# Attention scores from rounded parts, and one weight loaded a stage earlier into a place of its own

## What is computed

```python
ss = jnp.einsum('bghqd,bgqkd->bghqk', qb, kg) + bias_s      # selected keys
osel = jnp.einsum('bghqk,bgqkd->bghqd', masked_softmax(ss, ...), vg)
sw = jnp.einsum('bghqd,bgkd->bghqk', qb, kwb) + head_bias(rel_w)   # window keys
ow = jnp.einsum('bghqk,bgkd->bghqd', masked_softmax(sw, ...), vwb)
```

## Time and profile before

| what | value |
|---|---|
| median of 3 runs | 2342.91 us (2341.49 to 2344.74) |
| the profiled execution: its own time | 2339.77 us |
| its span, first to last instruction | 2337.7 us |
| granted TensorE clock, mean over the span | 0.986 of full |
| PE busy, share of the span | 95% |
| attention stage's 48 steps | about 783 to 931 us |
| state-space stage and what follows it | from 1183 us |
| mixture of experts | from about 1380 us to the end |

### The profile page before, as it was taken

How to read it: one execution, slowest core, us unless ns; L and a number is a source line. 1 busy time by engine, 2 the same in 40 slices (tenths; PEclk the granted TensorE clock), 3 DMA queues, 4 the chain that set the end, 5 groups by cost and what they waited for, 6 DMA issues and landing times. The chain is left out here.

```text
span 2337.7 us, 32450 instructions
## 1 busy us (share of the span) xinstructions
PE 2226.8 (95%) x13844; PEld 1652.4 (71%) x13844; DVE 820.4 (35%) x1668; ACT 504.4 (22%) x885; POOL 210.0 (9%) x173
## 2 busy tenths in 40 slices
PE   8999999999999998999989999999999999998987
PEld 5888888888888777878877876555565555555553
DVE  6453245243225688453256561111111111111113
ACT  3221333231223554242224220000000000000001
POOL 0640000011100000750000000000000000000000
PEclk9999999999999999999999999999999999999999
DMA  8633222354331100435163689999999999999997
GB/s 260 231 122 126 72 85 91 100 167 151 116 96 28 42 24 27 175 124 167 59 129 127 250 344 409 427 426 427 427 426 427 427 427 426 427 426 427 428 426 313
DMA packets 123829, 573.29 MB, mean 245 GB/s; under 512 B 30488, under 2 KB 44428, under 8 KB 97784
## 3 DMA queue, kind: packets, MB, share of 16 engines
q1 hardware_dynamic: 110468, 533.21, 58.2%
q0 software_dynamic: 12064, 33.79, 4.1%
q10 hardware_dynamic: 1152, 4.19, 0.5%
HBM read 543.63 MB, written 39.47 MB: 249 GB/s over the span
## 5 line engine op out<-in xcount | busy, mean ns | idle before, releaser
L525 PE MATMUL ps<-w_parts,u_parts 128*128 128x512 f32 (+2 forms) x1920 | 414.6, 376 | 2.9 <-DVE u_parts L713 2.6
L525 PEld LDWEIGHTS ps<-w_parts,u_parts 128*128 128x128 f32 x1920 | 349.2, 188 | 61.2 <-DVE u_parts L713 3.1
L3254 PE MATMUL ps<-mem,mem_u 128*64 128x256 f32 x2464 | 291.4, 390 | 4.5 <-issue 2.8
L490 DVE TENSOR_TENSOR w_parts<-w_raw,w_parts 128x2048 fp32r<-128x2048 f32 (+2 forms) x70 | 161.8, 2311 | 321.1 <-ACT w_parts L485 321.1
L3377 DVE TENSOR_TENSOR mem_c<-mem_c,ps 128x256 f32<-128x256 f32 x64 | 26.9, 421 | 684.9 <-PE ps L3254 678.7
L3254 PEld LDWEIGHTS ps<-mem,mem_u 128*64 128x64 f32 x2464 | 181.2, 135 | 110.2 <-issue 17.1
L485 ACT CAST w_parts<-w_raw 128x2048 fp32r<-128x2048 f32 (+2 forms) x70 | 128.6, 1837 | 399.4 <-PE ps L525 166.3
L3281 PE MATMUL ps<-mem,mem_c 128*64 128x512 f32 x624 | 194.7, 625 | 20.1 <-DMA mem<-in_expert_w_down 11.2
L1569 PE MATMUL ps<-w_parts,u_parts 128*128 128x512 f32 x768 | 181.6, 393 | 0.4 <-DVE u_parts L1598 0.4
L1569 PEld LDWEIGHTS ps<-w_parts,u_parts 128*128 128x128 f32 x768 | 142.2, 188 | 29.8 <-issue 0.8
L523 PE MATMUL ps<-u_parts,w_parts 128*128 128x512 f32 x672 | 154.5, 390 | 1.7 <-DVE w_parts L490 1.7
(11 more groups left out here) (447 smaller groups left out, 2675.3 us busy)
## 6 DMA issues: line engine op xcount, KB each, us to landing
mem<-in_expert_w_gate SPq DMA_DIRECT2D x39, 2048.0 KB, 35.6
mem<-in_expert_w_up SPq DMA_DIRECT2D x38, 2048.0 KB, 40.7
mem<-in_expert_w_down SPq DMA_DIRECT2D x37, 2048.0 KB, 40.9
mem_u<-in_expert_w_up SPq DMA_DIRECT2D x26, 2048.0 KB, 40.5
mem_u<-in_expert_w_down SPq DMA_DIRECT2D x19, 2048.0 KB, 42.1
mem_c<-in_expert_w_gate SPq DMA_DIRECT2D x13, 2048.0 KB, 36.0
mem_u<-in_expert_w_gate SPq DMA_DIRECT2D x12, 2048.0 KB, 36.6
w_raw<-in_od_w_in SPq DMA_DIRECT2D x21, 1024.0 KB, 5.1
```

What stands on the lines that cost most here:

```text
L490: dve.tensor_tensor(self.part(n, 1), self.raw(n), self.part(n, 0).bitcast(F32), ALU.subtract).then_inc(self.low, 1)
L525: mm = pe.matmul(out, u[:, x, ku, g.t * P:(g.t + 1) * P], w[y][:, kk, :], start=first, stop=last)
L3254: mm = pe.matmul(ps[SLOTS * h:SLOTS * (h + 1), bank, 0:256].rearrange("s (c j) -> s c j", j=2), x[:, kk, :], w[:, kk, :].rearrange("p (c h ...
```

## The change

Two parts.

**Attention.** The scores of heads 1 to 11, tiles 1 to 3, are made from rounded parts, three products each, where they were one float32 matmul. ACT rounds the four key matrices once, in step 0's turn, and each next head's queries in the turn of t=1; DVE makes the low parts, the keys' in step 1's turn, the queries' in the turn of t=2. For steps with t<2, ACT copies both transposed halves in one instruction, and DVE's copy is left out.

**Fourier output weight.** Chunk 4 gets a place of its own (`N0`), and SP issues its load in `ssm` right after the lag tables, ahead of the wait for `ft_ok`. The table `dft` moves to another free place. In `mix_mid` the copies of the state-space sums and the rounding of the weight take turns, on ACT and on DVE.

```diff
     def slot(self, n):
+        if n == FOURIER_CHUNK:
+            return N0
...
                     for i, kT in enumerate((k.ksT, k.kwT)):
-                        pe.matmul(k.ps[:, 2 * (u % 2) + i, 0:m], k.qT[:, h, t * P:(t + 1) * P], kT[:, g, 0:m],
-                                  start=True, stop=True).then_inc(scored, 1)
+                        if h == 0 or t == 0:
+                            mm = pe.matmul(o, k.qT[:, h, t * P:(t + 1) * P], kT[:, g, 0:m], start=True, stop=True)
+                        else:
+                            pe.wait_ge(k_low, 2 * NKV)
+                            pe.wait_ge(q_low, h)
+                            for x, z in PRODUCTS:
+                                mm = pe.matmul(o, q_parts[x][:, h % 2, t * P:(t + 1) * P],
+                                               k_parts[z][:, NKV * i + g, 0:m], start=x + z == 0, stop=x == 1)
+                        mm.then_inc(scored, 1)
...
             def take_turned(v):
-                act.wait_ge(turned, 2 * v + 1)
+                both = steps[v][1] < 2
+                act.wait_ge(turned, 2 * v + 1 + both)
...
+                if both:
+                    act.copy(pT[v % 2].rearrange("p (i w) -> p i w", i=2)[:, :, 0:w], k.ps[:, 4:6, 0:w]).then_inc(cop_a, 1)
...
                     exponential(u, 1)
+                    if u == 0:
+                        split_keys()
+                    if t == 1 and h + 1 < NH:
+                        split_head(h + 1)
...
+                    if u == 1:
+                        for i, kT in enumerate((k.ksT, k.kwT)):
+                            for g in range(NKV):
+                                dve.wait_ge(k_high, NKV * i + g + 1)
+                                dve.tensor_tensor(k_parts[1][:, NKV * i + g, :], kT[:, g, :],
+                                                  k_parts[0][:, NKV * i + g, :].bitcast(F32), ALU.subtract).then_inc(k_low, 1)
+                    if t == 2 and h + 1 < NH:
+                        dve.wait_ge(q_high, h + 1)
+                        dve.tensor_tensor(q_parts[1][:, (h + 1) % 2, :], k.qT[:, h + 1, :],
+                                          q_parts[0][:, (h + 1) % 2, :].bitcast(F32), ALU.subtract).then_inc(q_low, 1)
-                if 2 <= u < n + 2:
+                if 2 <= u < n + 2 and steps[u - 2][1] >= 2:
...
-    waves, dft = view(k, k.slot(first + 1) + 2048, NT, S), view(k, k.misc + 2080, 2 * P)
+    waves, dft = view(k, k.slot(first + 1) + 2048, NT, S), view(k, k.slot(first + 1), 2 * P)
...
                 sp.dma_start(T[SC * j:SC * (j + 1), :, :], kk[:, :, SC * (L - 1 - j):SC * (2 * L - 1 - j)]).then_inc(t_in, 16)
+            load_weights(k, sp, "ssm", first + 1)
             sp.wait_ge(ft_ok, 1)
...
             act.copy(ft[0], k.FT).then_inc(ft_high, 1)
-            k.last_sums(act)
             wait_chunk(k, act, first)
             for kk in range(4):
+                k.last_sum(act, kk)
                 act.copy(w4[0][:, kk, :], raw[0][:, kk, :]).then_inc(w4_high, 1)
...
-            k.last_sums_by_dve(dve)
...
+            k.last_sum_by_dve(dve, 0)
+            for kk in range(3):
+                k.last_sum_by_dve(dve, kk + 1)
+                four_low(kk)
+            four_low(3)
```

More of the change, by code:

```diff
@@ L66 @@
 ROUTE = Z0 + 16640
+FOURIER_CHUNK = 4
 def shape_constants():
@@ L1920, in nsa @@
     bias_loaded = [k.sem(f"nsa_bias{i}") for i in range(2)]
+    q_high, q_low, k_high, k_low = (k.sem("nsa_" + x) for x in ("q_high", "q_low", "keys_high", "keys_low"))
+    q_parts = [rounded(k, f"nsa_q_{x}", N0 + 1024 * i, 2, S) for i, x in enumerate(("high", "low"))]
+    k_parts = [rounded(k, f"nsa_keys_{x}", o, 2 * NKV, S) for x, o in (("high", Z0 + 11264), ("low", Z0 + 8192))]
+    PRODUCTS = ((0, 0), (0, 1), (1, 0))
     c_uses = [("score", t) for t in range(NT)]
@@ L1926, in nsa, with by_dve @@
             ("mix", 0): 11, ("turn", 2): 12, ("mix", 1): 13, ("turn", 3): 14, ("mix", 2): 16, ("mix", 3): 18}
+    def by_dve(v):
+        whole, rest = divmod(v + 1, NT)
+        return 2 * whole + max(0, rest - 2)
     def c_bank(use):
@@ L2020, in _ @@
                     for i, kT in enumerate((k.ksT, k.kwT)):
-                        pe.matmul(k.ps[:, 2 * (u % 2) + i, 0:m], k.qT[:, h, t * P:(t + 1) * P], kT[:, g, 0:m],
-                                  start=True, stop=True).then_inc(scored, 1)
+                        o = k.ps[:, 2 * (u % 2) + i, 0:m]
+                        if h == 0 or t == 0:
[7 more added lines that the diff above has]
+                        mm.then_inc(scored, 1)
                 if u >= 3:
@@ L2027, in _ @@
                     pe.wait_ge(cop_a, v + 1)
-                    pe.wait_ge(cop_v, v + 1)
+                    if by_dve(v):
+                        pe.wait_ge(cop_v, by_dve(v))
                     if v == 0:
@@ L2046, in _ @@
                         pe.wait_ge(exped, 2 * v + 1 + i)
-                        if v:
-                            pe.wait_ge(cop_v if i else cop_a, v)
+                        if i and v and steps[v - 1][1] >= 2:
+                            pe.wait_ge(cop_v, by_dve(v - 1))
+                        elif v:
+                            pe.wait_ge(cop_a, v)
                         for kt in range(t + 1):
@@ L2103, in _ @@
                     exponential(u, 1)
+                    h, t = steps[u]
+                    if u == 0:
+                        split_keys()
+                    if t == 1 and h + 1 < NH:
+                        split_head(h + 1)
                 if u == n - 2 * NT:
@@ L2154, in _ @@
                                                  st[:, u % 4, 0, b:b + 1]).then_inc(low, 1)
-                if 2 <= u < n + 2:
+                    if u == 1:
+                        for i, kT in enumerate((k.ksT, k.kwT)):
+                            for g in range(NKV):
+                                dve.wait_ge(k_high, NKV * i + g + 1)
[6 more added lines that the diff above has]
+                if 2 <= u < n + 2 and steps[u - 2][1] >= 2:
                     v = u - 2
                     w = (steps[v][1] + 1) * P
-                    if v >= 2:
-                        dve.wait_ge(mixed, v - 1)
+                    dve.wait_ge(mixed, v - 1)
                     dve.wait_ge(turned, 2 * v + 2)
@@ L2298, in ssm @@
     first = first_chunk(k, "mix_mid")
-    spare, lent = k.slot(first), k.slot(first + 2)
+    spare, lent = RING + 2 * SLOT, k.slot(first + 2)
     V = view(k, V0, 2 * 2, GP, (L + 1) * SC)
@@ L2431, in _, with last_sum, last_sum_by_dve @@
                 act.copy(CS[:, g, :], k.ps[:, g, :]).then_inc(cs_a, 1)
[L2433 to L2443, removed]
+        def last_sum(act, b):
+            act.wait_ge(y_mm, b + 1)
+            act.copy(y_bank(b, 0), y_sum(b, 0)).then_inc(y_a, 1)
+        def last_sum_by_dve(dve, b):
+            dve.wait_ge(y_mm, b + 1)
+            dve.tensor_copy(y_bank(b, 1), y_sum(b, 1)).then_inc(y_v, 1)
+        k.last_sum, k.last_sum_by_dve = last_sum, last_sum_by_dve
         @block.vector
@@ L2675, in _, with four_low @@
                                   ).then_inc(ft_low, 1)
-            k.last_sums_by_dve(dve)
-            for kk in range(4):
+            def four_low(kk):
                 dve.wait_ge(w4_high, kk + 1)
```

10 lines of the change are left out of this document (9 added, 1 removed).

## The result

The changed kernel takes 2346.61 us (median of 10 runs), the one before 2340.91 on the same chip (10 runs): ratio 1.0025, 95% interval 1.0016 to 1.0035. By that ratio it is 5.9 us slower (3.7 to 8.2), against a forecast of +0.3 within 2335 to 2349. The time lies in the range, and just beyond the 4.7 us that I called the edge of what can be told from no change. The profiled execution of after took 2344.14, with a span of 2342.1 and a mean clock of 0.988: 4.4 more than before.

A forecast was written before the change was run, and what follows sets the result against it. Experts wait on a weight stream, so earlier shifts move the end one for one; attention is bound by a ring through PE, DVE and ACT. Attention +4.8 and Fourier -4.5 give +0.3: 2340.1 profiled, 2343.2 median, range 2335 to 2349.

The forecast's parts named there:

- The ring: Attention heads: a dependency cycle through PE, DVE and ACT sets the period; 0.24, say 0.25 us longer a head, to 12.11.
- the copy's term: Attention ring: ACT's 512-wide copy takes 0.56 against 0.35, so +0.21 us a head ahead of the next head's first product.
- The start: Start of attention: key and query roundings queue on ACT, delaying the ring's first product by 2.3 us (bounds +1.2 to +2.8).
- Attention in sum: All of attention: ten longer heads, +2.5, and the start, +2.3, make +4.8 us, with bounds +2 to +8.
- PE decides: Rival in attention: PE's work sets the time, 11 heads save 0.80 each; whole -11.0 us, 2331.9; chance 0.14.
- The rival of the clock inside attention: Rival: PE's longer wait in each head drops the clock to 1.2 GHz; 11 heads cost 32 us, 2375; chance 0.08.
- The bank sums of PE come at its old pace, the last at 1247.15.: State-space stage before `mix_mid`: PE's sums keep their old timing, so PE starts the Fourier blocks at 1247.25, 3.3 us earlier.
- if the tables came late PE would wait inside `ssm`: Case in `ssm`: late lag tables would end PE's sums after 1247.15, costing one for one; forecast took cost nothing.
- The second part: Fourier weight loaded early for `mix_mid`: gives 4.5 us; 2.9 of the 4.6 block gain is the clock no longer falling.
- Blocks: Fourier blocks in `mix_mid`: the first ends at 1251.55, three more at 2.73 each end at 1259.7, instead of 1264.36.
- The trip of `ys`: Store and reload of `ys` around `mix_mid`: store 5.6, reload 5.4, done at 1259.8, just meeting PE's blocks.
- Whatever it gives or takes ahead of the experts moves the end one for one.: Experts' weight stream: starts when `mix_out` frees its first places, at an unchanged rate, so earlier shifts reach the end fully.

The follow-up runs named there:

- e11: Changed kernel with t=1's two halves copied by ACT and DVE as before; ratio 1.0018 to the kernel before.
- e7: Changed kernel with the query rounding moved to t=0's turn and DVE's subtraction to t=1's; ratio 1.0012 to the kernel before.
- e3: Changed kernel with all scores in float32 again, copies and roundings kept; ratio 1.0010 to the kernel before.
- e10: Changed kernel with wide copy only at t=0, query rounding at t=0, subtraction at t=1, keys' parts over five turns; ratio 0.9987 to the kernel before.
- e5: Kernel before plus ACT's wide copy at t=0 and the Fourier part, scores float32 without roundings; ratio 0.9975 to the kernel before.
- e4: The changed kernel as it is, run once more for a second trace; ratio 1.0023 to the kernel before.
- e1: Changed kernel without the Fourier part, attention's part alone; ratio 1.0033 to the kernel before.
- e2: Kernel before with the Fourier part alone, attention as before; ratio 0.9993 to the kernel before.
- e12: The kernel before, unchanged, run once more for a second trace; one run, 2342.26 us.
- e13: Kernel before with the Fourier part alone, run once more for a second trace; one run, 2338.24 us.
- e9: Changed kernel with the eight lag-table loads held back until PE's first state sums are half done; one run, 2340.70 us.

## Why the prediction was right in its range and low by 5.6

- **The ring.** Right in structure and in size. Predicted 12.11, measured 12.10; the copy's term 0.21 is e11's, the subtraction holds DVE its 0.60 (e7), the scores' saving stays outside (e3), M(1)'s wait is 1.20 (predicted about 1.5). That wait came out shorter because the rounded products are dearer than scaled: S(2) takes 1.14 (857.13 to 858.27) where I had 1.02, and a head saves 0.5, not 0.80.
- **The start.** Predicted +2.3, measured 7.05 - 4.82 = +2.23.
- **Attention in sum.** Predicted +4.8, measured +4.6 at the first load of `ssm`.
- **The rival "PE decides".** It needs an unloaded ring. With rounded scores it did not come, even e10 waits for ACT; with float32 scores and one wide copy it did (e5). **The rival of the clock inside attention.** It stayed at 1.00 through waits of 1.20 in every head; in e7 it fell once, behind a wait of 2.32.
- **The failed step: "The bank sums of PE come at its old pace, the last at 1247.15."** I allowed for late tables ("if the tables came late PE would wait inside `ssm`") but not for PE's own instructions. In their place the runs showed a gap of 3.88 where before has 1.16, and low clock behind it. The bank sums came 3.4 behind attention's shift, in e4 and e1 8. It is an effect of attention's part, not of the Fourier part: e1 has it without the Fourier load, e2 lacks it with the load. In times, e3 against the changed kernel puts it at 3 to 4 us.
- **The second part.** Blocks: right, over 12.3 after the last sum (predicted 12.55), at clock 1.00. The trip of `ys`: from the last sum to the transposes 13.15, predicted 12.65; the store took 6.8 and not 5.6. So it gave 3.9 in this pair of traces, where I had 4.5. But 2.9 of mine was a fall of the clock that e12, the same kernel as before, does not have. Against e12, e2's transposes come 2.7 sooner (79.81 - 77.14), e13's only 0.2 sooner, and whole runs of e2 show 1.7, not clear of the noise. The term should have been at most about 2 to 2.7.
- **"Whatever it gives or takes ahead of the experts moves the end one for one."** The pair of traces agrees at its end (+4.1 and +4.4), but not on the way (+2.9 at the load of 1402.40). It holds to some 2 us, and only where `mix_out`'s clock does the same in both, which is not a given.
- **The range.** That it held is in part luck. The time of before on which it stands was 2342.91 (3 runs), and the ten runs gave 2340.91. Measured from the same base the forecast missed by 5.6 us, and the two terms that missed, the gap and the clock's fall booked as a gain, were not among those that the range was made from.

The sum with the measured terms: +4.6 in attention and its start, +3.4 to +4 for the gap, -1.7 to -2.7 for the Fourier part: +5.3 to +6.9, where +5.9 was measured.

What stays open: why the gap is 3.88 in one trace of the changed kernel and 6.28 in another (the packet came 9.0 and 11.4 after the first product); what holds the packet up among the small ones; how often the clock falls at each of its places; and the 3.5 us ahead of attention.

## What to carry to other kernels

Walk the ring through all engines, with what each instruction holds its engine and not only its duration: that gave this change's cost to 0.01 us a head. An operation is free in the turn in which its engine waits and costs its full length one turn later, as the subtraction did; and one engine's wide copy in place of another's late one can be worth more than cheaper arithmetic, which pays only once the engine that does it no longer waits in the ring. An edit that adds instructions to a saturated engine can move the moments at which its next instructions must arrive in a stage that it does not touch, here 260 us later: look for "issue" gaps of one engine near small-packet loads, and see in the DMA view whether an instruction packet stands behind them. And take a second trace of the kernel before, before you book a clock's fall as a gain.

## What the hardware showed beyond expectation

- PE's instructions come over a DMA queue of their own kind, in packets of some 16 KB (by estimate 256 instructions), and such a packet due among loads of small packets comes 2.7 to 5 us later: gaps of 2.8 to 6.6 in the six traces with all the rounded scores, 0.55 when the loads are held back (e9). The Trainium skill (DMA: Bandwidth & Descriptors, Queues, rings and completion order) says that a DMA engine takes turns between the queues that have work, a packet at a time. A whole queue ahead of the instructions would then not hold them up; the trace shows a delay of several packets' time, and no run here shows in which order the engines took them.
- Six rounded products took 1.48 at 512 columns (860.27 to 861.75 in after), 1.14 at 384, against 1.72 and 1.29 for the two float32 ones: 14% and 12% less.
- The granted clock fell behind an idle time of 1.24 in five traces and not in nine others, at the same instructions. At the first Fourier block it held through 3.08 once (e12), where it fell with 3.41 (before) and with 2.98 (e1).
